# Two transformer blocks with routed experts: the scatter split into fp32r parts, two weight units opened ahead of each branch, weights laid out by units, and two narrow gemms merged into wider ones

## The reference, cut to what matters

```python
logits = (xt @ w_router).astype(jnp.float32)
top_v, top_e = lax.top_k(logits, TOP_K)
gates = jax.nn.softmax(top_v, axis=-1)
...
yb = lax.map(run, (buf.reshape(n_blocks, EXPERT_BLOCK, D), block_e)).reshape(P, D)   # (silu(x @ w1) * (x @ w3)) @ w2
y = jnp.zeros((T, D), x.dtype).at[stok].add(yb[dest] * sg[:, None].astype(x.dtype))
...
e = jax.nn.sigmoid(x @ w_ple_gate[i]) * (p[i] @ w_ple_proj[i])
x = _layernorm(DEEPNORM_ALPHA * x + f + e, ln_ffn_g[i], ln_ffn_b[i])
```

## Time and profile before

| | us |
|---|---|
| three runs: median, lowest, highest | 2822.3, 2821.92, 2826.16 |
| the profiled execution's own time | 2819.11 |
| its span in the profile | 2817.0 |
| busy in it: TensorE | 2726.6 (97%) |
| VectorE | 2112.9 (75%) |
| ScalarE | 1627.6 (58%) |
| mean granted clock of TensorE | 0.99 |

### The profile page before, as it was taken

How to read it: one execution, slowest core, us unless ns; L and a number is a source line. 1 busy time by engine, 2 the same in 40 slices (tenths; PEclk the granted TensorE clock), 3 DMA queues, 4 the chain that set the end, 5 groups by cost and what they waited for, 6 DMA issues and landing times.

```text
span 2817.0 us, 44738 instructions
## 1 busy us (share of the span) xinstructions
PE 2726.6 (97%) x19124; PEld 2316.3 (82%) x19124; DVE 2112.9 (75%) x2115; ACT 1627.6 (58%) x1630; POOL 141.4 (5%) x152
## 2 busy tenths in 40 slices
PE   8999999999999999999999999999999999989999
PEld 7877898887778787878878787778778988867997
DVE  6677655657779888888989898877766867766685
ACT  4454443455467676776767676746545645554563
POOL 1000000000000000000000000000430000051000
PEclk9999999999999999999999999999999999999999
DMA  7345555545369999999999999963115555312552
GB/s 218 131 155 168 179 180 174 173 151 166 112 242 340 348 343 344 347 344 334 354 330 357 331 353 350 364 194 122 62 62 173 180 180 170 120 63 83 167 180 105
DMA packets 360333, 616.15 MB, mean 219 GB/s; under 512 B 13776, under 2 KB 117200, under 8 KB 360112
## 3 DMA queue, kind: packets, MB, share of 16 engines
q1 hardware_dynamic: 355216, 598.61, 60.8%
q0 software_dynamic: 4896, 14.36, 2.2%
HBM read 611.88 MB, written 1.05 MB: 218 GB/s over the span
## 4 chain that ended last, share of the span: by engine, by line
PE 82%; DVE 10%; ACT 5%; issue 2%; DMA 0%; SPq 0%; DVEq 0%; ACTq 0%
PE ps L697 24%; PE ps L698 23%; PE ps L699 23%; DVE wlo L1725 3%; ACT whi L1319 1%; PE ps L1033 1%; PE ps L1179 1%; PE ps L1002 1%; PE ps L1023 1%; ACT s L1610 1%; PE ps L1158 1%; PE ps L1190 0%; DVE s L2084 0%; PE ps L818 0%; PE ps L897 0%
## 5 line engine op out<-in xcount | busy, mean ns | idle before, releaser
L1725 DVE TENSOR_TENSOR wlo<-raw,whi 128x2048 fp32r<-128x2048 f32 (+2 forms) x588 | 1304.1, 2223 | 417.4 <-ACT whi L1319 409.6
L1319 ACT ACTIVATE whi<-raw 128x2048 fp32r<-128x2048 f32 (+2 forms) x588 | 1092.9, 1859 | 409.4 <-PE ps L699 390.6
L697 PE MATMUL ps<-whi,xTh 128*128 128x512 f32 (+4 forms) x1464 | 578.5, 395 | 7.7 <-DVE g L2208 2.9
L698 PE MATMUL ps<-wlo,xTh 128*128 128x512 f32 (+4 forms) x1464 | 568.5, 388 | 0.0
L699 PE MATMUL ps<-whi,xTl 128*128 128x512 f32 (+4 forms) x1464 | 568.5, 388 | 0.0
L698 PE MATMUL ps<-xTl,whi 128*128 128x256 f32 x1480 | 418.2, 283 | 0.0
L697 PE MATMUL ps<-xTh,whi 128*128 128x256 f32 x1480 | 417.4, 282 | 0.0
L699 PE MATMUL ps<-xTh,wlo 128*128 128x256 f32 x1480 | 417.2, 282 | 0.0
L697 PEld LDWEIGHTS ps<-whi,xTh 128*128 128x128 f32 x1464 | 279.2, 191 | 70.2 <-issue 7.3
L699 PEld LDWEIGHTS ps<-whi,xTl 128*128 128x128 f32 x1464 | 279.0, 191 | 61.3
L698 PEld LDWEIGHTS ps<-wlo,xTh 128*128 128x128 f32 x1464 | 279.5, 191 | 56.3
(11 more groups left out here) (557 smaller groups left out, 3490.2 us busy)
## 6 DMA issues: line engine op xcount, KB each, us to landing
raw<-in_expert_w_dram SPq DMA_DIRECT2D x336, 1024.0 KB, 5.8
raw<-in_w_in_dram SPq DMA_DIRECT2D x76, 1024.0 KB, 5.2
raw<-in_w_up_dram SPq DMA_DIRECT2D x44, 1024.0 KB, 5.1
raw<-in_dense_w_dram SPq DMA_DIRECT2D x32, 1024.0 KB, 5.1
raw<-in_w_down_dram SPq DMA_DIRECT2D x20, 1024.0 KB, 5.3
raw<-in_w_out_dram SPq DMA_DIRECT2D x16, 1024.0 KB, 5.0
raw<-in_w_branch_diff_dram SPq DMA_DIRECT2D x8, 1024.0 KB, 5.0
raw<-in_w_ple_gate_dram SPq DMA_DIRECT2D x8, 1024.0 KB, 4.9
```

Source lines behind the costliest of these rows:

```text
L697: self.e.matmul(out, ah, bh, start=start, stop=False)
L698: self.e.matmul(out, ah, bl, start=False, stop=False)
L1319: self.e.activation(self.m.hi[u % NHL][:, 0:n], self.m.raw[u % NRAW][:, 0:n], ACT.Copy) \
L1725: self.e.tensor_tensor(self.m.lo[u % NHL][:, 0:n], self.m.raw[u % NRAW][:, 0:n], self.m.hi[u % NHL][:, 0:n].bitcast(F32), ALU.subtract) \
```

## The change

- **Scatter.** The output of w2 is split into a high and a low fp32r part, kept in the part of `hTe` that the product has already read; the scatter is a high and a low fp32r product of `selT`, the transposed selection without the gates. VectorE multiplies with the gate when it adds to `y`. The first half of the output is split at a new step "rest", two units into the second w2 product. There are two `selT`, and the turn of expert ex + 1 stands between the two scatters of expert ex, ahead of the branch on every engine.
- **Opening.** `open_expert` issues three of the four contraction steps of both units of the first w1 block ahead of the branch; the fourth step of each follows behind it.
- **Layout.** The host lays out all weights in the order and shape of the units, so that a unit is one contiguous piece and a partition's row of it (8 KB in a unit of 1 MB) is contiguous.
- **Router.** The 8 router columns and the 1024 gate columns stand in one matrix, taken as three gemms of 344 columns (two units each). The split of x moves ahead of them (step "rows"), and the gated embedding is added in three pieces at "rank", "counts" and "gather".
- **Decay columns.** The 32 columns and z become two gemms of 272 columns (two units each), at the places of the old two.

The diff, cut to its core:

```diff
-            self.sel, self.selg = t("sel", [128, 2, 256], F32R, c0), t("selg", [128, 2, 256], F32, c0)
-            self.selgT = t("selgT", [128, 2, 256], F32, c0)
+            self.sel = t("sel", [128, 2, 256], F32R, c0)
+            self.selT = [t(f"selT{k}", [128, 2, 256], F32R, c0) for k in range(2)]
...
-            o += self.gemm(("rt",), "route", m.xT, a["router_w"][0], "a", 8, 0, 8, xt)
-            o += [("rank",)] + pg[0][0:1] + [("count",)] + pg[0][1:2] + [("route",)] + pg[1][0:1] + [("counts",)]
-            o += pg[1][1:2] + [("gather", 0)]
+            W = a["w_route_gate"]
+            pr = [self.gemm(("pr", c), "route", m.xT, W, "a", 8, THIRD * c, THIRD, xt) for c in range(3)]
+            o += [("rows",)] + pr[0] + [("rank",)] + pr[1][0:1] + [("count",)] + pr[1][1:2] + [("route",)] + pr[2][0:1]
+            o += [("counts",)] + pr[2][1:2] + [("gather", 0)]
...
-            o += [("begin", ex), ("turn", ex)]
+            o += [("turn", 0)] if ex == 0 else []
+            o += [("begin", ex)]
...
-            o += e2[0][ex == 7:] + e2[1][0:n] + [("scatter", ex, 0)] + e2[1][n:] + [("scatter", ex, 1), ("finish", ex)]
+            o += e2[0][ex == 7:] + e2[1][0:2] + [("rest", ex, 0)] + e2[1][2:n] + [("scatter", ex, 0)] + e2[1][n:]
+            o += [("turn", ex + 1)] if ex < 7 else []
+            o += [("scatter", ex, 1), ("finish", ex)]
...
-        z = self.gemm(("z", l), "conv", m.xT, W, "a", 8, 2336, 512, xt)
-        bd = self.gemm(("bd2", l), "conv", m.xT, W, "a", 8, 2304, 32, xt)
+        zb = [self.gemm(("zb", l, k), "conv", m.xT, W, "a", 8, 2304 + 272 * k, 272, xt) for k in range(2)]
...
-        begun = j == 0 and g == self.opened
+        begun = g == self.opened
...
-        self.e.wait_ge(*self.at("lo", u))
         v = lambda t: t[:, 0:4 * w].rearrange("p (c n) -> p c n", c=4)
-        wh, wl = v(self.m.hi[u % NHL]), v(self.m.lo[u % NHL])
-        for k in range(3):
-            self.mm3(ps[:, 0:w], xh[:, k, 0:128], xl[:, k, 0:128], wh[:, k, :], wl[:, k, :], k == 0, False)
+        for j in range(2):
+            u = self.p.unit[g, j]
+            self.e.wait_ge(*self.at("lo", u))
+            wh, wl = v(self.m.hi[u % NHL]), v(self.m.lo[u % NHL])
+            for k in range(3):
+                self.mm3(ps[:, 0:w], xh[:, 4 * j + k, 0:128], xl[:, 4 * j + k, 0:128], wh[:, k, :], wl[:, k, :],
+                         j == k == 0, False)
...
+        e.wait_ge(*self.at("hiT", "ev", "e2", ex, cb))
+        for q in range(2):
+            for s in range(self.tiles):
+                e.matmul(ps[:, q * 512:q * 512 + 512], T[:, s, q * 128:q * 128 + 128], high[:, s, :], start=(s == 0), stop=False)
         e.wait_ge(*self.at("ev", "e2", ex, cb))
         for q in range(2):
             for s in range(self.tiles):
-                ins = e.matmul(ps[:, q * 512:q * 512 + 512], m.selgT[:, s, q * 128:q * 128 + 128], m.hb[:, cb, s, :],
-                               start=(s == 0), stop=(s == self.tiles - 1))
+                ins = e.matmul(ps[:, q * 512:q * 512 + 512], T[:, s, q * 128:q * 128 + 128], low[:, s, :], start=False,
+                               stop=(s == self.tiles - 1))
...
-            e.tensor_tensor(yy, yy, bands(self.psum("sc", *a)), ALU.add).then_inc(*self.up("d_moe", ("y",) + a))
+            for t in range(2):
+                ins = e.scalar_tensor_tensor(yy[:, t, :], bands(self.psum("sc", *a))[:, t, :], m.gate[:, t, a[0]:a[0] + 1],
+                                             yy[:, t, :], ALU.mult, ALU.add)
...
-            e.tensor_scalar(m.selg[:, t, :], m.iota[:, :], m.pos[:, t, ex:ex + 1], m.gate[:, t, ex:ex + 1], ALU.is_equal,
-                            ALU.mult)
...
-            src = W[k0 * 128:(k0 + kc) * 128, n0:n0 + w].rearrange("(c p) n -> p c n", p=128)
-            dst = m.raw[u % NRAW][:, 0:kc * w].rearrange("p (c n) -> p c n", c=kc)
-            e.dma_start(dst, src).then_inc(*self.c.up(f"raw{u % NRAW}", ("raw", u), by=16))
+            src = self.a["units"][o:o + 128 * kc * w].rearrange("(p n) -> p n", p=128)
+            o += 128 * kc * w
+            e.dma_start(m.raw[u % NRAW][:, 0:kc * w], src).then_inc(*self.c.up(f"raw{u % NRAW}", ("raw", u), by=16))
```

More of the change, by code:

```diff
@@ L663, in do @@
             self.gather(*a)
+        elif what == "turn":
+            self.turn(*a)
         elif what == "across":
@@ L962, in expert @@
     def expert(self, ex, j0, j1):
-        self.turn(ex)
         self.opened = ("e1", ex, 0)
@@ L969, in open_expert @@
     def open_expert(self, g):
-        G, u = self.p.gemms[g], self.p.unit[g, 0]
+        G = self.p.gemms[g]
         ps, (xh, xl), w = self.fill(g, ("ev",) + g), G.x, G.w
@@ L1008, in turn @@
         e, m = self.e, self.m
-        ps = self.fill(("turn", ex), ("selgT", ex))
+        e.wait_ge(*self.at("sel", ex))
+        ps = self.fill(("turn", ex), ("selT", ex))
         for s in range(2):
@@ L1418, in do @@
             e.wait_ge(*self.at("full", "turn", a[0]))
-            e.activation(m.selgT[:, :, :], bands(self.psum("turn", a[0]), 4)[:, 0:2, :], ACT.Copy) \
-                .then_inc(*self.up("a_moe", ("selgT", a[0])))
+            if a[0] > 1:
+                e.wait_ge(*self.at("full", "sc", a[0] - 2, 1))
+            e.activation(m.selT[a[0] % 2][:, :, :], bands(self.psum("turn", a[0]), 4)[:, 0:2, :], ACT.Copy) \
+                .then_inc(*self.up("a_moe", ("selT", a[0])))
         elif what == "across":
@@ L1426, in do @@
                 .then_inc(*self.up("a_moe", ("hiT", "hTe", ex, cb)))
+        elif what == "rest":
+            e.wait_ge(*self.at("unit", self.p.unit[("e2", a[0], 1), 0]))
+            self.expert_high(*a)
         elif what == "rms":
@@ L1810, in do @@
             self.branch_gate(("bo", a[0], 1))
+        elif what == "rows":
+            self.rows_low()
         elif what == "rank":
             self.rank()
+            self.gated(0)
         elif what == "route":
@@ L1817, in do @@
         elif what == "counts":
-            self.rows_low()
+            self.gated(1)
             self.select(0)
@@ L1822, in do @@
         elif what == "gather":
+            if a[0] == 0:
+                self.gated(2)
             for d0 in (0, 4):
@@ L1837, in do @@
             e.wait_ge(*self.at("full", "sc", *a))
-            e.tensor_tensor(yy, yy, bands(self.psum("sc", *a)), ALU.add).then_inc(*self.up("d_moe", ("y",) + a))
+            for t in range(2):
+                ins = e.scalar_tensor_tensor(yy[:, t, :], bands(self.psum("sc", *a))[:, t, :], m.gate[:, t, a[0]:a[0] + 1],
+                                             yy[:, t, :], ALU.mult, ALU.add)
+            ins.then_inc(*self.up("d_moe", ("y",) + a))
+        elif what == "rest":
+            e.wait_ge(*self.at("unit", self.p.unit[("e2", a[0], 1), 0]))
+            self.expert_low(*a)
         elif what == "rms":
@@ L2269, in product, with gated, expert_low @@
                 .then_inc(*self.up("d_gate", ("ev",) + g))
+    def gated(self, c):
+        e, m = self.e, self.m
+        o, n0 = (8, 0) if c == 0 else (0, THIRD * c - 8)
+        gE, cols = m.gE1[:, :, o:THIRD], slice(n0, n0 + THIRD - o)
+        e.wait_ge(*self.at("ev", "pp", 1, 1 if c else 0))
+        e.wait_ge(*self.at("ev", "pr", c))
+        e.tensor_tensor(gE, m.gP1[:, :, :, :].rearrange("p t c n -> p t (c n)")[:, :, cols], gE, ALU.mult).then_inc(*self.up("d_ple"))
+        e.wait_ge(*self.prev)
+        e.scalar_tensor_tensor(m.y1[:, :, cols], m.x[:, :, cols], ALPHA, gE, ALU.mult, ALU.add) \
+            .then_inc(*self.up("d_ple", ("py", 1, c)))
+    def expert_low(self, ex, cb):
+        g, n, (high, low) = ("e2", ex, cb), self.tiles, self.m.expert_sum(cb)
+        self.e.wait_ge(*self.at("hiT", "ev", *g))
+        self.e.tensor_tensor(low[:, 0:n, :], bands(self.psum(*g))[:, 0:n, :], high[:, 0:n, :].bitcast(F32), ALU.subtract) \
+            .then_inc(*self.up("d_moe", ("ev",) + g))
     def branch_gate(self, g):
@@ L2814, in program @@
         m = Memory(nc, ctx)
-        k = Kernel(Plan(a, m), m, a, out, Counts(lambda n: ctx.enter_context(nc.semaphore(n))))
+        plan = Plan(a, m)
+        size = sum(128 * kc * w for _, _, kc, _, w in plan.units)
+        a["units"] = nc.dram_tensor("in_units_dram", (size,), F32, kind="ExternalInput").ap()
+        k = Kernel(plan, m, a, out, Counts(lambda n: ctx.enter_context(nc.semaphore(n))))
         for engine in (Tensor, Scalar, Vector, Pool, Sync):
@@ L2839, in _, with laid_out @@
             Tensor(k, e).run()
+    return plan.units
+def laid_out(units):
+    import numpy as np
+    rows = [W[k0 * 128:(k0 + kc) * 128, n0:n0 + w].reshape(kc, 128, w).transpose(1, 0, 2).reshape(-1)
+            for W, k0, kc, n0, w in units]
+    return np.concatenate(rows)
 def thresholds():
@@ L2898, in prepare @@
     out = nc.dram_tensor("out_0_dram", (1, 256, 1024), F32, kind="ExternalOutput").ap()
-    program(nc, a, out)
+    arrays["in_units_dram"] = laid_out(program(nc, a, out))
     return arrays
```

113 lines of the change are left out of this document (70 added, 43 removed).

## The result

| | before | after |
|---|---|---|
| median of 15 runs each, us | 2822.3 | 2831.4 |
| profiled execution's own time | 2819.1 | 2828.7 |
| its span | 2817.0 | 2826.6 |
| busy: TensorE | 2726.6 | 2701.4 |
| busy: VectorE | 2112.9 | 2119.4 |

The ratio of after to before is 1.0025, with a 95% interval from 1.0017 to 1.0033: slower by 7 us by the ratio (9 by the medians), where 11 less were forecast. TensorE is busy 25 us less, and the kernel is slower all the same. Of the runs further down, one execution of `a_one_open` took 6706 us and is left out of its ratio.

A forecast was written before the change was run, and what follows sets the result against it. TensorE was taken to bound the experts, VectorE the second block's mixer. Experts +1.0, router -7.5, decay columns -4.0 and layout -0.5 gave -11 us, so a median of 2811; own range 2804 to 2817, 8 in 10 2801 to 2820.

The forecast's parts named there:

- Would the shorter seam be stopped by the branch instead?: At a seam: TensorE, released 2.45 us after the first scatter product (T), needs code at T+6.0, has work until T+7.2.
- Rival 3: At each expert's branch: larger weight packets delay VectorE's code past 3.6 us; with 2.5 the kernel takes 2831; chance 0.07.
- The second opening: At each expert's opening: 18 products issued ahead cover the branch for 4.2 us instead of 2.1.
- Scatter and fourth unit: At the seams: scatter saves 1.57 us, low part waits 0.55, fourth unit costs 1.2; seven seams +1.3 us.
- First expert: First expert, where nothing hides the branch: 1.38 us of issue goes, 1.1 comes, -0.3 us.
- the 1.38 of issue: TensorE's wait for issue at the first expert's branch, 1.38 us, expected to go.
- the fourth unit's 1.1: At each expert's fourth unit, eight times: TensorE waits 1.1 us for its low part after two opening units.
- Router: Router: 144 products of 344 columns replace 48 of 8 and 96 of 512; -7.5 us, bounds -4 and -8.7.
- The half clock: Router: the stretch at 1.2 GHz behind the narrow products goes, with some 3 us of the difference.
- the reading of the counts: Router: it remains, with 1.05 us of idle time; together with the counting products 2.0 us.
- Decay columns: Second block's mixer: shorter VectorE splits save 2.35 us per layer; -4 us for two layers, bounds 0 and -10.
- Layout: Start of the program: longer rows may bring the first unit sooner; 0.5 us taken, bounds 0 and 2.5.

The follow-up runs named there:

- a_one_open: The changed kernel with one unit opened ahead of the branch instead of two; ratio 1.0052 to the kernel before.
- c_pause: The changed kernel with one weight load per seam issued one unit later; 2817.8 us, ratio 0.9971 to the kernel before.
- e_two_open_pause: The kernel before with two opening units, weights laid out by units and one load per seam issued a unit later; ratio 1.0026.
- b_new_layout: The kernel before with only the weights laid out by units, in rows of 8 KB; ratio 0.9994.
- a_old_layout: The changed kernel with the weights read from their own arrays again, in rows of 1 to 2 KB; ratio 1.0046 to the kernel before.
- a_rows2k: The changed kernel with each unit still one contiguous piece, but in rows of 2 KB and less; ratio 1.0050 to the kernel before.
- c_halves: The changed kernel with each unit loaded in two transfers of half the size; ratio 1.0047 to the kernel before.
- d_router_decay: The kernel before with the change's router, decay columns and layout, the experts as before; 2809.9 us, ratio 0.9946.
- e_pad: The changed kernel with 40 more products of 8 columns on TensorE at the very start; ratio 1.0045 to the kernel before.

## Why the prediction was wrong, point by point

- **The step that failed** is the one under "Would the shorter seam be stopped by the branch instead?": released at T+2.45, TensorE "needs code at T+6.0". It took the bare 3.5 us of the first expert for the seams. At the first expert the DMA engines were idle when the code was asked for; at a seam they stream at 0.94, and the packet stands behind every load issued before it. The code came at T+8.5. The seam before had hidden this with 0.1 to 0.6 us to spare (packet at T+3.0 to T+3.5, 2.4 more, work until T+6.0). Cost: 0.9 to 1.5 us at six seams and 6.8 at one, where a further packet was waited for, which the prediction had no term for: 13.8 of the 17 us. The rest goes with them: at each seam the pitch is 0.3 us over the 129.0 of `c_pause` plus its wait, and at the long one 1.6, where the stretch behind it ran at a lower clock (granted 0.78 over 1590 to 1602 us):

```profile
1590.00:1602.00 12.00, 5.22 (x22) 4.15 (x21) 4.34 (x5) 0.97 (x1) 0.00 (x0) 0.78 0.49 181
```

- **Rival 3** had the right sign and kind and nearly the time (2831), but the wrong reason and the wrong engine: it let VectorE's jump come late, and in the fence of the first seam VectorE goes from its additions (936.96) to its next split (939.73) without a gap, while TensorE waits. Larger packets do nothing; the order of request and load does. That its number was met is luck.
- **The second opening** as cover for the branch: at T+7.1 its work ends, so it would have been enough had the code come at 6.0. Behind the old fp32 scatter it also delays the request itself (`e_two_open_pause`), which was not in the prediction; behind the new one hardly.
- **Scatter and fourth unit:** the low part waited 0.34 for 0.55, the opening came at T+2.91 for 2.95, the fourth unit waited 0.88 for 1.1, at six experts and not at eight. With the load moved the pitch is 129.0 as forecast. The working has two values for the scatter's gain, 0.84 (from T+3.79 to T+2.95) and 1.57 - 0.55 = 1.02, and the sum goes by the larger; measured it is 0.88. At a pitch of +0.2 seven seams make +1.5, for the +1.3 of the forecast: that step was right for a kernel whose code is in time.
- **First expert:** the 1.38 of issue is gone, as forecast. The stretch gave 1.0 us and not 0.3: the fourth unit's 1.1 did not come in full. VectorE's issue went from 3.38 to 4.03, and TensorE waited 0.27 and 0.37 for its low parts.
- **Router:** -6.8 for -7.5. The half clock went; the reading of the counts took 2.45 us of idle time for 1.05, which the forecast had left as it was; that is more than the 0.7 that is missing.
- **Decay columns:** forecast -4, measured -0.5 with the last expert's tail. The mechanism held: TensorE waited 8.57 for 3.75 and the stretch from the first to the last transposes of the convolution fell by 3.2 and 2.3 us (56.2 to 53.0, 56.2 to 53.9), for 2.35 forecast. What was given back lies in part in the delta rule (+2.9 over both layers, with waits for issue of 2.0 and 1.6 at L1288). But one trace is too little to price a stretch this long: from the last scatter to TensorE's last product `b_new_layout` took 984.5 for the 983.4 of the kernel before, and `a_old_layout`, `a_rows2k`, `c_pause` and `c_halves` took 983.2 to 986.3 for the 982.8 of the change, all with TensorE instructions unchanged. So -0.5 and the -4.7 of `d_router_decay` are not told from the forecast -4 by these traces, and the cause of the difference stays open.
- **Layout:** -0.5 as forecast, all at the start. Every kernel with rows of 8 KB in one transfer (`e_pad` aside) has its first product with weights at 15.0 to 15.3 us, the others at 15.9 to 16.2. By the router the traces of either kind are spread over 0.6 to 1.5 us, so what is left there of the gain is not measured well.

What stays open: why the further packet comes when it does and not sooner, why the issue waits of the delta rule change between kernels with the same TensorE instructions, and what the decay columns are worth. The reach of some 20 products is an estimate from one position.

## What to carry to other kernels

A runtime branch in a kernel that streams weights is a DMA request. Look up its packet in the windows of the instruction queues, write down by how much it is ahead of the next load, and count every change that moves the last wait ahead of the branch, or adds work between it and the branch, against that margin. If it is late, hold back one load rather than add products: here that was worth some 15 us. Look also whether a second packet is needed soon behind the branch. And price a branch at a place where the DMA engines are as busy as where it will stand.

## What the runs showed of the hardware that was not expected

- A code packet of 16 KB waits for the loads issued ahead of it: it comes 2.8 us later for one further load of 1 MB (T+3.0 to T+3.5 against T+5.8 to T+6.3). Two transfers for one (T+6.5 to T+7.0) or rows of 2 KB for 8 KB (T+6.2 to T+7.5 in `a_rows2k`) bring it no sooner.
- From the start of the packet to the first product behind the branch it is 2.4 us, with idle DMA engines (first expert, 817.57 to 820.01) or busy ones (seams: 2.4 to 2.7; 4.1 where two packets stood side by side).
- TensorE's sequencer does not take a branch as soon as its waits are over: with 18 products and 4 transposes ahead of it the packet landed 3.2 us after the last wait (T+1.7 to T+4.9) with idle DMA engines, where it is 1.5 us with 9 products ahead.
- A wait can stand behind the next 16 KB of code too: 6.8 us at one branch, ending 2.4 us behind the start of that packet. The same instructions, moved by 40 products, lost it there and got one of 2.7 at another branch.
